# A hybrid decoder step: the sample's page lookup in four chunks on POOL, conv additions with a pause, conv products spread over more jobs

## The reference, cut to what matters

```python
# prompt: 512 tokens; sample: 8 sequences x 8 new tokens over 4096 cached positions in pages of 128
a_glu, b_glu, q, k, v, qi, ki, wi, g_c, g_a = split(h @ w_in)          # D = 1024, fp32
glu = a_glu * sigmoid(b_glu)                                            # 512 channels
c = silu(layer_norm(causal_depthwise_conv(concat(prefix, glu), conv_w, conv_b)))   # width 31
conv_branch = c @ w_conv_out
# indexer scores, then per query the best keys: 256 of 4104 (sample), 128 of 512 (prompt)
scores = sum_h relu(qi_h . ki) * w_h * IDX_SCALE
idx = top_k(where(key_pos <= q_pos, scores, -inf), k)
phys = page_table[idx // 128]; off = idx % 128                          # sample only
o = softmax(q . K[phys, off]) . V[phys, off]                            # chosen keys alone
mix = (sigmoid(g_c) * conv_branch + sigmoid(g_a) * (o @ w_attn_out)) @ w_o
x1 = layer_norm(alpha * h + mix); y = layer_norm(alpha * x1 + hier_moe(x1) + ple)
```

## Time and profile before

| what | us |
|---|---|
| three runs: median (lowest to highest) | 1848.52 (1848.18 to 1849.42) |
| the profiled execution: its own time | 1854.38 |
| its span | 1852.3 |
| PE / DVE / ACT / POOL busy | 1395.8 / 776.6 / 451.3 / 511.6 |
| mean granted TensorE clock | 0.853 |

### The profile page before, as it was taken

One profiled execution on the slowest core, in us unless ns is written; L12 is line 12 of the kernel. 1 busy time (PEld: TensorE's weight loads), 2 busy tenths in 40 slices (PEclk: granted clock), 3 DMA queues, 4 the chain that ended last, 5 costly groups with the idle time before them and its releaser, 6 DMA issues. The chain is left out here.

```text
span 1852.3 us, 18901 instructions
## 1 busy us (share of the span) xinstructions
PE 1395.8 (75%) x7353; PEld 793.2 (43%) x7353; DVE 776.6 (42%) x1306; ACT 451.3 (24%) x900; POOL 511.6 (28%) x444
## 2 busy tenths in 40 slices
PE   5799996679419995677677689938988687689960
PEld 5435553445215553343233236827764243344420
DVE  3269999996795401222222223133242111112218
ACT  2621455562215514322111111111111010011110
POOL 2100699993100000034334310000042331333320
PEclk9999997799755697788888799966989897899985
DMA  7411211112300010055656652081118988888803
GB/s 227 172 32 62 69 46 45 49 51 66 114 4 1 1 34 23 12 182 204 233 199 228 219 184 80 23 316 53 58 36 338 363 325 319 329 320 317 316 12 143
DMA packets 87318, 268.78 MB, mean 145 GB/s; under 512 B 16047, under 2 KB 50599, under 8 KB 76663
## 3 DMA queue, kind: packets, MB, share of 16 engines
q1 hardware_dynamic: 50832, 157.25, 22.9%
q0 software_dynamic: 33920, 107.06, 16.4%
q10 hardware_dynamic: 2479, 3.27, 0.6%
HBM read 292.58 MB, written 23.00 MB: 170 GB/s over the span
## 5 line engine op out<-in xcount | busy, mean ns | idle before, releaser
L787 PE MATMUL ps<-arena 128*128 128x64 f32 (+3 forms) x1216 | 341.7, 448 | 14.5 <-ACT arena L1275 6.2
L787 PEld LDWEIGHTS ps<-arena 128*128 128x128 f32 (+1 forms) x1216 | 189.9, 199 | 166.5 <-issue 155.1
L1099 PE MATMUL ps<-arena 128*64 128x256 f32 x1568 | 208.6, 413 | 61.2 <-DMA arena<-in_w_gu,arena 59.4
L695 POOL DMA_INDIRECT arena<-in_kv,arena x128 | 121.7, 951 | 357.5 <-ACT arena L1165 186.8
L673 POOL TENSOR_TENSOR arena<-arena 128x816 f32<-128x816 f32 x116 | 206.2, 1777 | 23.7 <-ACT arena L1183 7.6
L1099 PEld LDWEIGHTS ps<-arena 128*64 128x64 f32 x1568 | 115.7, 148 | 149.1 <-DMA arena<-in_w_gu,arena 69.8
L793 PE MATMUL ps<-arena 128*128 128x256 f32 (+5 forms) x640 | 138.8, 381 | 17.0 <-ACT arena L1292 8.6
L1183 ACT ACTIVATE arena<-arena 128x816 f32<-128x816 f32 x120 | 116.5, 975 | 89.7 <-POOL arena L673 85.0
L793 PEld LDWEIGHTS ps<-arena 128*128 128x128 f32 (+1 forms) x640 | 113.2, 204 | 42.5 <-issue 11.4
L1165 ACT ACTIVATE arena<-ps 128x256 f32<-128x256 f32 (+5 forms) x148 | 61.2, 418 | 277.0 <-PE ps L959 66.9
L748 POOL DMA_INDIRECT scr_ypair<-arena x49 | 50.0, 1020 | 260.7 <-ACT arena L1406 256.3
(11 more groups left out here) (301 smaller groups left out, 1690.0 us busy)
## 6 DMA issues: line engine op xcount, KB each, us to landing
arena<-in_w_gu SPq DMA_DIRECT2D x32, 2048.0 KB
arena<-in_w_dn SPq DMA_DIRECT2D x32, 1024.0 KB
arena<-in_w_in SPq DMA_DIRECT2D x20, 1024.0 KB, 5.5
arena<-in_w_o SPq DMA_DIRECT2D x4, 1024.0 KB, 5.0
arena<-in_w_pg SPq DMA_DIRECT2D x4, 1024.0 KB, 6.9
arena<-scr_ypair SPq DMA_DIRECT2D x4, 1024.0 KB, 6.6
arena<-in_x_prompt SPq DMA_DIRECT2D x4, 512.0 KB, 11.6
scr_h<-arena SPq DMA_DIRECT2D x4, 512.0 KB, 3.6
```

The costliest lines, as they stand in the source:

```text
L695: pl.indirect_dma_start(kv(g, 2 * j + t), None, I["kv"], bass.IndirectOffsetOnAxis(ap=offs[:, t, n:n + 1], axis=0)).then_inc(kv_in[g % 2 * ...
L787: mm = nc.tensor.matmul(out, w[:, k], hT[:, k, a:b], start=(k == 0), stop=(k == KC - 1))
L1099: mm = nc.tensor.matmul(PS[2 + p % 2][64 * half:64 * half + 64, 0:2 * P], xT[:, p % 3, j, 64 * h:64 * h + 64], w[:, k, half, :], start=(k ...
```

## The change

The page lookup moves from DVE to POOL and is cut into four chunks of 80, 80, 64 and 32 list entries. Behind the round that completes a chunk, DVE computes that chunk's pages, offsets and keys and gives `page_ready`. POOL compares the chunk's pages with all 32 page numbers into a scratch area (32 tensor_scalars), and adds the 32 results pairwise (five additions of 16, 8, 4, 2 and 1 times the chunk's width); these five wait for each other. Chunk 0 stands ahead of the first conv addition, chunks 1, 2 and 3 ahead of additions 24, 38 and 42. Behind chunk 3 and ahead of addition 42 POOL waits for `lists_ready`. DVE waits for all four chunks behind its last round and goes on as before. The products stand two behind a job whose kind ends in P and one behind every other, so that they reach 61 jobs further, into the scores and the attention.

```diff
--- before.py
+++ after.py
...
+CHUNKS = [(0, 80), (80, 160), (160, 224), (224, TOPS)]
+MAP_AT = {1: 24, 2: 38, 3: 42}
 CLEN = PRE + NP + NB * (PRE + NQ) - PRE
 PRODUCTS = {}
 _n = 0
 for _j in JOBS[NUM[("bP", 1, 0)]:]:
-    _take = min(3, (2 if NUM[_j] < NUM[("aS", 1, 1)] else CC) * CW - _n)
+    _take = min(2 if _j[0][-1] == "P" else 1, (2 if NUM[_j] < NUM[("aS", 1, 1)] else CC) * CW - _n)
     PRODUCTS[_j] = range(_n, _n + _take)
     _n += _take
+assert _n == CC * CW
...
         prod = view(ki_at + 2 * (CLEN + PRE), (3, CLEN + PRE))
+        hot_at = ki_at + 5 * (CLEN + PRE)
+        assert hot_at + PAGES * 80 <= q_at
...
+        page_ready = sem("page_ready")
+        hot_step = sem("hot_step")
+        row_ready = sem("row_ready")
         conv_ready = sem("conv_ready")
...
                 pl.wait_ge(glu_ready, 1 + 3 * c + 2)
                 nc.gpsimd.tensor_copy(gluS[:, c, :, PRE:], gs[:, c, :].rearrange("p (b q) -> p b q", b=NB)).then_inc(glu_ready, 1)
 
+            def physical_rows(i):
+
+                c0, c1 = CHUNKS[i]
+                w = c1 - c0
+                hot = view(hot_at, (PAGES, w))
+                pl.wait_ge(page_ready, i + 1)
+                if i:
+                    pl.wait_ge(row_ready, i)
+                n = 5 * i
+                for page in range(PAGES):
+                    ins = nc.gpsimd.tensor_scalar(hot[:, page], lst[:, 0, c0:c1], float(page), ptf[:, page:page + 1], ALU.is_equal, ALU.mult)
+                ins.then_inc(hot_step, 1)
+                half = PAGES // 2
+                for j in range(4):
+                    pl.wait_ge(hot_step, n + 1 + j)
+                    nc.gpsimd.tensor_tensor(hot[:, 0:half], hot[:, 0:half], hot[:, half:2 * half], ALU.add).then_inc(hot_step, 1)
+                    half //= 2
+                pl.wait_ge(hot_step, n + 5)
+                nc.gpsimd.tensor_tensor(lst[:, 2, c0:c1], hot[:, 0], hot[:, 1], ALU.add).then_inc(row_ready, 1)
+
             def conv(c):
                 a = acc[:, c % 2]
                 for w in range(1, CW):
                     k = c * (CW - 1) + w - 1
+                    for i, at in MAP_AT.items():
+                        if k == at:
+                            physical_rows(i)
+                    if k == MAP_AT[3]:
+                        pl.wait_ge(lists_ready, 1)
                     p = prod[:, k % 3]
                     pl.wait_ge(prod_ready, c * CW + w + 1)
                     if w > 1:
...
             for c in range(0, CC, 2):
                 gated(c)
                 gated(c + 1)
+                if c == 0:
+                    physical_rows(0)
                 conv(c)
                 conv(c + 1)
             pl.wait_ge(conv_ready, CC)
...
             for c in range(4):
                 dve.wait_ge(summed, 4 * c + 4)
                 step(nc.vector.tensor_scalar(work[:, c * 512:(c + 1) * 512], PS[4 + c][:, :], ISC, None, ALU.mult))
+            L = [lst[:, i, :] for i in range(8)]
+            V = nc.vector
+            page, key, row = L[0], L[1], L[2]
+            step(V.tensor_copy(ptf, pti))
             for r in range(TOPS // 8):
                 m = vals[:, r * 8:r * 8 + 8]
-                step(nc.vector.max(m, work))
-                nc.vector.max_index(idxu[:, r * 8:r * 8 + 8], m, work)
-                step(nc.vector.match_replace(work, m, work, TAKEN))
-
-
-            L = [lst[:, i, :] for i in range(8)]
-            V = nc.vector
-            page, key, row, tmp = L[0], L[1], L[2], L[3]
-            V.tensor_copy(ptf, pti)
-            step(V.tensor_scalar(L[4].bitcast(U32), idxu, 6, None, ALU.logical_shift_right))
-            V.tensor_copy(page, L[4].bitcast(U32))
-            step(V.tensor_scalar(L[5].bitcast(U32), idxu, 63, None, ALU.bitwise_and))
-            V.tensor_scalar(key, idxu, 2.0, C["par"], ALU.mult, ALU.add)
-            V.tensor_scalar(L[6], L[5].bitcast(U32), 2.0, C["par"], ALU.mult, ALU.add)
-            step(V.tensor_scalar(row, page, 0.0, ptf[:, 0:1], ALU.is_equal, ALU.mult))
-            for p in range(1, PAGES):
-                step(V.tensor_scalar(tmp, page, float(p), ptf[:, p:p + 1], ALU.is_equal, ALU.mult))
-                step(V.tensor_tensor(row, row, tmp, ALU.add))
+                step(V.max(m, work))
+                V.max_index(idxu[:, r * 8:r * 8 + 8], m, work)
+                step(V.match_replace(work, m, work, TAKEN))
+                for c0, c1 in CHUNKS:
+                    if c1 == r * 8 + 8:
+                        sub = idxu[:, c0:c1]
+                        V.tensor_scalar(L[5].bitcast(U32)[:, c0:c1], sub, 63, None, ALU.bitwise_and)
+                        step(V.tensor_scalar(L[4].bitcast(U32)[:, c0:c1], sub, 6, None, ALU.logical_shift_right))
+                        V.tensor_copy(page[:, c0:c1], L[4].bitcast(U32)[:, c0:c1]).then_inc(page_ready, 1)
+                        V.tensor_scalar(key[:, c0:c1], sub, 2.0, C["par"], ALU.mult, ALU.add)
+                        step(V.tensor_scalar(L[6][:, c0:c1], L[5].bitcast(U32)[:, c0:c1], 2.0, C["par"], ALU.mult, ALU.add))
+            dve.wait_ge(row_ready, len(CHUNKS))
             step(V.scalar_tensor_tensor(row, row, float(PG), L[6], ALU.mult, ALU.add))
 
             v0, k0, reven = vals[0:NS], key[0:NS], row[0:NS]
```

## The result

The changed kernel takes 1889.57 us (median of 4 runs, 1884.45 to 1897.36) against 1848.35 (4 runs on the same chip): a ratio of 1.0228, 95% interval 1.0189 to 1.0268. I forecast slower, and 1864.5 with a range of 1838 to 1882; the direction holds, the size does not, and the time lies above the range. The profiled execution took 1892.24 (span 1890.4), 37.9 above that of before.

The account below looks back on a forecast made before the run. TensorE was taken to be held by products up to "offs", then DVE's prompt selection and the attention units bound. Terms -37 (up to "offs"), +31 (scores), +22 (units) gave +16: 1864.5 us, range 1838 to 1882.

Parts of the forecast that it names:

- What bounds the kernel: Up to "offs", TensorE is held by products waiting 85.0 us for POOL's additions; DVE's late lists cost nothing by themselves.
- When the lists are ready: End of DVE's list code: at 364 us (357 to 377) instead of 448, the last chunk taking POOL 12 us.
- the earlier chunks (14 us of POOL each) are hidden: POOL's lookups before the last chunk: cost TensorE nothing, since it may run four jobs ahead of ScalarE.
- a dearer lookup: Rival: POOL tensor_scalar takes 0.55, last chunk 20, lists 8 to 9 late, 1873 us; chance 0.15 shared with other dearer cases.
- TensorE up to offs: TensorE no longer held in the pairs, stands from 348 to 367.3, "offs" drained at 433.6 instead of 470.5.
- my -37: Gain up to the drain of "offs": 37 us (44 with lists at 357, 24 at 377).
- Prompt scores: After "offs", 24 products make score operations wait for additions: +11.7, +9.6 and +10 in three tiles, sum +31 us.
- Attention units: The last 20 products stretch first exponential to pt 6 from 12.2 to 34 us: +22 (15 to 28).
- From there all distances are as before: Behind pt 6 in the attention units: nothing of the change is left, so no cost.
- The sum: Whole kernel: -37 + 31 + 22 = +16 us, 1864.5 on the median.
- The faster one: Rival: score operations don't wait for POOL, scores and units cost 28 in all, 1832 to 1840 us; chance 0.18.

Follow-up runs that it names:

- the first edit alone: The kernel before with only the products thinned to two or one a job, lookup left on DVE, no pause: 1841.06 us, ratio 0.9951.
- Half the comparisons: The changed kernel with 16 instead of 32 comparisons in each chunk, the other 16 rows set to zero: 1860.89 us, ratio 1.0045.
- the wide ones: The changed kernel with each chunk's 32 comparisons replaced by three wide operations (subtract, compare with 0, multiply): 1871.29 us, ratio 1.0093.
- no pause: The changed kernel without POOL's wait for `lists_ready` between the last chunk and addition 42: 1875.84 us, ratio 1.0131.
- the first half alone, well placed: The kernel before with products two or one a job, from "offs" on 8, 10 and 12 ahead of the selections, then one a unit from the ninth: 1792.83 us.

## Why the prediction was right or wrong

**What bounds the kernel: right.** TensorE was held by the products and the late lists cost nothing: with the first edit alone "offs" comes 62.7 us earlier, with the lookup alone 100 us later. (With the products thinned, TensorE is at "offs" 2.3 us ahead of DVE's lists.)

**"When the lists are ready": this step failed, by the size of its main term.** I took 0.28 us for a POOL tensor_scalar with a comparison and a product and bounded it by 0.55; it takes 0.46 from one to the next with 32 columns, 0.57 with 64, 0.62 with 80. I put it between operations that are simpler (a copy, an addition, a tensor_scalar of two integers); the lookup has 128 of them, so this error is worth 37 us of POOL (14.8 + 18.2 + 20.0 + 20.0 = 73 us in the four chunks against 128 x 0.28 = 36). Two parts reached the lists. The last chunk took 18.2 us instead of 12 (comparisons 14.8 for 9.0, additions 3.4 for 2.75): +6. And "the earlier chunks (14 us of POOL each) are hidden" was false: they took 26.6, 26.5 and 23.7, POOL was behind, and the last chunk began 8.9 us after its pages. The pages came at 345.9 instead of 341: +5. Sum 20.1 us: 384.1 instead of 364. My rival "a dearer lookup" had the first part alone and hence 1873. Half the comparisons and the wide ones show the whole: lists at 365.2 and 366.5 put "offs" at 435.7 and 436.7.

**"TensorE up to offs": right from the pause on, wrong ahead of it.** I had TensorE no longer held up to 348. It was held twice before, 7.1 us up to 300.8 and 8.65 up to 350.6, because the products waited while POOL did the second and third chunk: on this side too they were not hidden. Here that cost nothing, since the pause held TensorE afterwards in any case; that these two gaps don't show in the time is luck. TensorE stood until lists plus 3.05 us (I had 3.3), and it was 68.2 us from there to the drain of "offs" (I had 66.3). In all kernels with the pause and this order of products ahead of it "offs" ends 70.2 to 71.6 us after the lists (ready at 365.2, 366.5, 376.1, 384.1, 385.4): what the lists lose, TensorE loses. Where my -37 stood, -15.2 was measured; 20.1 of the 21.7 is the lists' delay.

**Prompt scores: the wait is right, the +30.2 against +31 partly luck.** The first maximum came 19.75 us after "offs", by starts, where I had 17.3; so the first tile paid 14.1 (I had 11.7), the tiles with 384 and 512 columns 6.5 (9.6) and 9.6 (10). One by one, the seven score operations of the second tile took 0.62 us three times and 1.87 to 2.15 four times, those of the third 0.75 twice and 2.00 to 2.29 five times: the ones beside additions cost the 1.9 to 2.3 that I gave. In the first tile they took 0.67 to 0.95, and the two operations behind the second tile's scores took 1.7 us instead of 4.1; the sum came out because these misses cancel. The neighbour I argued from, a tensor_tensor beside additions, was the right one: the scalar_tensor_tensor takes 1714 ns at 512 columns in the mean of the third tile and 752 where no addition runs beside it. By the Trainium skill, page SBUF — State Buffer, section "SBUF: two separate sides", a DVE instruction with two SBUF inputs and a GpSimd instruction that reads SBUF lock each other out, whichever starts first; the trace agrees, with these numbers. Selections did not notice POOL (695 ns in both), as forecast, and moving the products into them took 27 of the 30 us away.

**Attention units: right up to pt 6, short behind it.** From the first exponential to pt 6 it was 32.3 us (I had 34, against 12.2 before): +20.0 instead of +22. "From there all distances are as before" was wrong by 4 us: the last drain ends 86.0 us after pt 6's start instead of 82.1. Two windows, after and before, of the 40 us from pt 6 on:

```profile
598.00:638.00 40.00, 37.11 (x100) 18.86 (x101) 20.88 (x63) 20.04 (x65) 13.77 (x13) 0.50 0.30 106
```

```profile
563.00:603.00 40.00, 40.00 (x110) 20.63 (x109) 20.93 (x69) 20.13 (x67) 0.00 (x0) 0.50 0.00 1
```

At the same granted clock, 0.50 (1.2 GHz), TensorE does 100 matmuls instead of 110. POOL's last additions and the gathers' descriptors (13.8 us busy) fall into this window where it had nothing; which of them it is, no run tells apart.

**The sum.** By stages I had too little by 21.7 - 0.8 - 2.0 + 3.8 - 0.8 (the rest) = 21.9, and by the profiled executions 37.9 - 16 = 21.9. Nine tenths of it is the lists' delay. The medians differ by 25.1 from my 1864.5; the other 3.2 are the profiled execution of before, which lay 5.9 above its median while that of the changed kernel lies 2.7 above its own.

**The rivals.** The faster one needed score operations that do not wait for POOL; they do. Its number, that the selections offer 60 us of POOL's time, was the way to gain: 30 additions put there cost 0.4 to 3.3 us.

## What to carry to other kernels

Before moving an operation to another engine, price its exact form there, not a neighbour's: a tensor_scalar of 32 to 80 columns on GpSimd cost a fixed part of some 290 ns that outweighed its width, and work "hidden" on an engine that others already wait for is not hidden. Where a wait is taken off one stage by spreading the work over later ones, ask for each later stage which engine is last there; here the same product cost about 1.1 us beside small DVE operations and about 0.1 us or less beside MAX8 and MATCH_REPLACE8. And undo each half of a combined change: here the first half alone, well placed, gives 0.970, and no run with the second half was as fast.

## What the runs showed of the hardware that I had not expected

- GpSimd: tensor_scalar, compare and multiply by a column, busy 398, 505, 558 ns for 32, 64, 80 fp32 columns; compare alone 408 at 80; a compare over 2560 elements 6.68 us (2.6 ns each), a subtraction with broadcast operands over as many 4.47 us (1.75 ns each).
- The lock is not only for two sources: one-source DVE operations meet GpSimd's additions too, though not each: a copy of 256 columns took 1.89, 0.28 and 1.72 us in a row (no pause), and a cast of 32 columns 1.22 in the changed kernel, where with POOL idle it took 0.18 (half the comparisons). By the Trainium skill, page SBUF — State Buffer, section "Who interferes with whom", copy, cast and tensor_scalar can take the shared ports in their two-port modes if their operands allow it; the trace agrees, with these numbers. MAX8 and MATCH_REPLACE8 took the same with additions and without.
- TensorE's granted clock was 0.50 through the 109 us of scores, in which it was busy for 35.3, and still 0.50 in the 40 us behind pt 6, where it was busy for 37.1.
